# The samples' convolution, forget sums and value pages of a hybrid decoder step, moved to earlier places

## What is computed

```
mod = silu(c) @ w_mod + b_mod                      # six shift, scale and gate vectors
proj = modulate(rms(x)) @ w_in                     # columns: delta-rule heads, forgetting-attention heads
q,k,v = silu(causal_conv(proj[q,k,v], state_conv)) # 4 taps; samples: 3 older rows come from state_conv
o_gdn = gated_delta_chunked(l2norm(q), l2norm(k), v, g, beta, state_delta)
s = fq . fk / 8 + F_q - F_k ; F = cumsum(log forget)   # over all 2048 cached tokens and the new one
o_fox = softmax(s) @ v                             # samples: cached pages through page_table
x = x + g1 * ([o_gdn, o_fox] @ w_out)
x = x + g2 * peer(modulate(rms(x)))                # 8 heads x 16 experts per token, gathered rows of u and v
```

## Time and profile before

| | |
|---|---|
| median of three runs | 2023.49 us |
| the profiled execution's own time | 2020.36 us |
| its span, first to last instruction | 2017.2 us |
| TensorE busy, share of the span | 1651.2 us, 82% |
| VectorE busy | 1344.7 us, 67% |
| GpSimd busy | 816.4 us, 40% |
| ScalarE busy | 675.8 us, 34% |
| DMA | 722.49 MB, mean 358 GB/s |
| mean granted TensorE clock | 0.916 of full speed |

### The profile page before, as it was taken

How to read it: one execution, slowest core, us unless ns; L and a number is a source line. 1 busy time by engine, 2 the same in 40 slices (tenths; PEclk the granted TensorE clock), 3 DMA queues, 4 the chain that set the end, 5 groups by cost and what they waited for, 6 DMA issues and landing times.

```text
span 2017.2 us, 26386 instructions
## 1 busy us (share of the span) xinstructions
PE 1651.2 (82%) x8416; PEld 886.5 (44%) x8416; DVE 1344.7 (67%) x3103; ACT 675.8 (34%) x1971; POOL 816.4 (40%) x602
## 2 busy tenths in 40 slices
PE   6997989987968897776799787679978888887776
PEld 4444456654655553343355244335533443332233
DVE  4245767653468876666887666688768677775754
ACT  2111232121134452333445333344533333442332
POOL 0188664213014443343444234444434443444441
PEclk9998999987989997899899879889978999999999
DMA  7378657975679999999999999999999999999996
GB/s 309 111 261 286 223 172 242 320 240 189 204 304 418 420 417 423 422 421 421 406 391 406 423 413 422 421 401 402 392 415 405 422 421 419 420 422 421 420 408 276
DMA packets 130437, 722.49 MB, mean 358 GB/s; under 512 B 17288, under 2 KB 19017, under 8 KB 58357
## 3 DMA queue, kind: packets, MB, share of 16 engines
q0 software_dynamic: 75024, 545.82, 65.7%
q1 hardware_dynamic: 55277, 175.00, 24.1%
HBM read 711.77 MB, written 9.09 MB: 357 GB/s over the span
## 4 chain that ended last, share of the span: by engine, by line
PE 36%; DMA 31%; DVE 14%; issue 7%; SPq 5%; POOL 4%; ACT 3%; DVEq 0%; POOLq 0%; ACTq 0%
PE bank L493 35%; DMA R<-in_peer_uv,R 17%; DMA RING<-in_peer_uv,R 11%; DVE RING L2299 3%; SPq L2570 2%; SPq L2624 2%; DVE R L2299 2%; POOL MV L2486 1%; PE bank L500 1%; ACT R L1407 1%; DMA R<-in_x_prompt 1%; POOL R L2486 1%; POOL R L2556 1%; DMA RING<-samp_d 1%; ACT R L1417 1%
## 5 line engine op out<-in xcount | busy, mean ns | idle before, releaser
L2556 POOL DMA_INDIRECT RING<-in_peer_uv,R x390 | 442.2, 1134 | 663.5 <-PE bank L493 541.1
L493 PE MATMUL bank<-RING,R 128*64 128x512 f32 (+2 forms) x1560 | 516.7, 668 | 190.2 <-ACT R L1407 177.8
L2299 DVE SCALAR_TENSOR_TENSOR RING<-RING,MV 128x1024 f32<-128x1024 f32 x288 | 351.7, 1223 | 186.1 <-DMA RING<-in_peer_uv,R 167.0
L493 PE MATMUL bank<-R 128*128 128x128 f32 (+6 forms) x2184 | 404.5, 385 | 80.4 <-ACT R L1407 69.4
L493 PEld LDWEIGHTS bank<-R 128*128 128x128 f32 (+3 forms) x2184 | 261.2, 188 | 246.3 <-issue 236.5
L493 PEld LDWEIGHTS bank<-RING,R 128*64 128x64 f32 (+2 forms) x1560 | 159.0, 161 | 446.0 <-issue 433.8
L1417 ACT ACTIVATE R<-R 128x2 f32<-128x2 f32 x256 | 51.9, 203 | 705.5 <-DVE RING L2299 562.2
L2556 POOL DMA_INDIRECT R<-in_peer_uv,R x130 | 153.8, 1183 | 218.7 <-PE bank L493 200.9
L2299 DVE SCALAR_TENSOR_TENSOR RING<-RING,R 128x1024 f32<-128x1024 f32 x96 | 117.3, 1222 | 57.3 <-DMA RING<-in_peer_uv,R 49.7
L2299 DVE SCALAR_TENSOR_TENSOR R<-R,MV 128x1024 f32<-128x1024 f32 x96 | 117.5, 1224 | 55.2 <-DMA R<-in_peer_uv,R 49.2
L493 PE MATMUL bank<-HT,RING 128*128 128x512 f32 x320 | 140.7, 597 | 0.0
(11 more groups left out here) (340 smaller groups left out, 1888.7 us busy)
## 6 DMA issues: line engine op xcount, KB each, us to landing
R<-in_peer_wq SPq DMA_DIRECT2D x12, 2048.0 KB
RING<-in_w_mod SPq DMA_DIRECT2D x11, 2048.0 KB, 9.8
MV<-in_cache_k SPq DMA_DIRECT2D x88, 256.0 KB, 3.9
R<-in_cache_v SPq DMA_DIRECT2D x84, 256.0 KB, 3.6
R<-in_w_out SPq DMA_DIRECT2D x6, 2048.0 KB
MV<-in_cache_v SPq DMA_DIRECT2D x44, 256.0 KB, 3.8
R<-in_cache_k SPq DMA_DIRECT2D x40, 256.0 KB, 3.6
RING<-in_peer_uv,R POOLq DMA_INDIRECT x390
```

Of the source, the lines that this page charges most:

```text
L493: i = nc.tensor.matmul(out, lhsT, rhs, start=start, stop=stop, **k)
L2299: V.scalar_tensor_tensor(u, u, 1.0, H2HIGH if s_ % 2 and n < PAIRED * PH else H2[n // PH % 2], ALU.mult, ALU.mult, accum_out=DOT[:, n % 4, ...
L2556: nc.gpsimd.indirect_dma_start(UV[g % UN], None, a["peer_uv"][0], bass.IndirectOffsetOnAxis(ap=idx, axis=0)).then_inc(S(f"uv_in{g % UN}"), 16)
```

## The change

- **Samples' convolution.** It moves from GpSimd to VectorE, and from 8 rows of 512 columns to four blocks of 32 rows (8 used) of 128 columns. The weights and older rows are laid out so in two new inputs, zero in the unused rows, and loaded once, after the samples' rows of x. ScalarE copies the raw columns with one instruction (PSQ) for each of q, k, v. `sample_taps` (behind key group 4) multiplies and adds the older three rows, `sample_conv` (unit 1) adds the newest; silu comes at unit 2.
- **Forget sums.** TensorE's transposes and sums go before the fq projection and behind it; VectorE's parts stand behind key groups 0, 6, 7, 8, 9, 10 and 11.
- **New scores.** They are made behind key group 14; TensorE spreads them and the new log forgets with products by ones (`new_rows`), and VectorE copies them in convolution block 9. The trip through DRAM goes.
- **Softmax and values.** `sample_scores` comes at unit 0, `sample_probs` at 8, value group 0 at unit 10, up to group 15 at 25; groups 16 to 31 keep their places. SRULE_AT begins at 7 instead of 16.
- **SyncE.** Value groups 0 and 1 are loaded right behind the modulation biases; `sample_state_in` stands before `next_mod(5)`, ahead of the loop.
- **Tails.** TensorE's `tail_turns` and VectorE's `tails_out` stand ahead of the loop instead of in unit 0.

```diff
-SRULE_AT = (16, 19, 22, 25, 29)
+SRULE_AT = (7, 10, 13, 16, 20)
...
-        SCW = part(R2, 0, 2048, n=4, c=512)
-        SST = part(R2, 10760, 1536, n=3, c=512)
-        PSC = R2[:, 9224:9224 + CONV]
+        SCW = part(R2, 9216, 1536, j=TAPS, c=3 * P)
+        SST = part(R2, 10760, 1152, j=3, c=3 * P)
+        PSQ = part(R2, 8704, 384, n=3, c=P)
+        PSC = part(R2, 5696, 384, n=3, c=P)
...
-            return 18 + n if n < 16 else FOX_STEPS + (max(0, (n - 16) // 2 - 1) if LATE == 1 else (n - 16) * 7 * LATE // 16)
+            return 10 + n if n < 16 else FOX_STEPS + (max(0, (n - 16) // 2 - 1) if LATE == 1 else (n - 16) * 7 * LATE // 16)
...
+            forget_turns()
...
+                if name == "fq":
+                    forget_sums()
...
+            def new_rows():
+
+                pe.wait_ge(S("new_rows"), 2)
+                b = take_bank("new", "D")
+                mm(b[:, 0:64], ones[0:NB, :], NEW_LOGF.rearrange("p b h -> p (b h)"))
+                mm(b[0:1, 64:128], ones[0:NB, 0:1], NEW_SCORE.rearrange("p h b -> p (h b)"), sem=full("new"))
...
-            steps = {0: tail_turns, 1: forget_turns, 3: forget_sums, 10: sample_max_turn, 12: sample_max_spread, 16: sample_sums}
+            steps = {1: sample_max_turn, 3: sample_max_spread, 7: sample_sums}
...
+            tail_turns()
...
-                sample_rows((name, 4), g * 512, ACT.Copy)
-                act.sem_inc(S("sample_raw"), 1)
+                b = full_bank(act, (name, 4))
+                A(PSQ[:, g, :], b[:, 0:P], ACT.Copy).then_inc(S("sample_raw"), 1)
+                act.wait_ge(S("sample_raw"), g + 1)
+                act.sem_inc(free((name, 4)), 1)
...
-                if u == 12:
-
-                    act.wait_ge(S("sconv_done"), 3)
-                    A(PSC[0:NB, :], PSC[0:NB, :], ACT.Silu).then_inc(S("sconv_silu"), 1)
-                if u == 14:
+                if u == 2:
+                    act.wait_ge(S("sconv_done"), 1)
+                    A(PSC, PSC, ACT.Silu).then_inc(S("sconv_silu"), 1)
+                if u == 5:
...
+            def forget_pages(last, first):
+
+                for g in range(last, first - 1, -1):
+                    settle()
+                    step(V.tensor_tensor(TP[:, :, :, g], TP[:, :, :, g], TP[:, :, :, g + 1], ALU.add))
+
+            def forget_total():
+
+                settle()
+                step(V.tensor_tensor(flat(LP[:, :, :, 0:15]), flat(LP[:, :, :, 0:15]), flat(TP[:, :, :, 1:16]), ALU.add))
...
+            def sample_taps():
+
+                dve.wait_ge(S("sconv_in"), 32)
+                step(V.tensor_tensor(SST, SST, SCW[:, 0:3, :], ALU.mult))
+                for j in (1, 2):
+                    settle()
+                    step(V.tensor_tensor(SST[:, 0, :], SST[:, 0, :], SST[:, j, :], ALU.add))
+
+            def new_scores():
+
+                dve.wait_ge(S("sample_cols"), 12)
+                T8 = CACT[0:NB, 0, :]
+                step(V.tensor_tensor(T8, PS[0:NB, COL_FQ:COL_FQ + 512], PS[0:NB, COL_FK:COL_FK + 512], ALU.mult))
+                settle()
+                step(V.tensor_reduce(SN[0:NB, :], T8.rearrange("p (h d) -> p h d", h=8), AXX, ALU.add))
+                settle()
+                V.tensor_tensor(NEW_SCORE, SN[0:NB, :].rearrange("p (h o) -> p h o", o=1).to_broadcast([NB, 8, NB]),
+                                ident[0:NB, 0:NB].rearrange("p (o b) -> p o b", o=1).to_broadcast([NB, 8, NB]), ALU.mult).then_inc(S("new_rows"), 1)
+
+            among_keys = {0: forget_turned, 4: sample_taps, 6: forget_after, 7: lambda: forget_pages(14, 12), 8: lambda: forget_pages(11, 9),
+                          9: lambda: forget_pages(8, 5), 10: lambda: forget_pages(4, 0), 11: forget_total, 14: new_scores}
             for n in range(KEYS_BEFORE - 1):
                 key_group(n)
+                if n in among_keys:
+                    among_keys[n]()
             b = full_bank(dve, "gab")
             step(V.tensor_copy(GATE[:, 0:4, :], b[:, 0:4 * GATES_W].rearrange("p (t h) -> p t h", h=GATES_W)))
...
+            V.tensor_tensor(NEW_LOGF, ident[0:NB, 0:NB].rearrange("p (b o) -> p b o", o=1).to_broadcast([NB, NB, 8]),
+                            LOGF[0:NB, 4:5, :].to_broadcast([NB, NB, 8]), ALU.mult).then_inc(S("new_rows"), 1)
...
+                if cb == 9:
+                    b = full_bank(dve, "new")
+                    step(V.tensor_copy(LNB, b[:, 0:64]))
+                    dve.wait_ge(S("scores_cleared"), 1)
+                    V.tensor_copy(SC[0:1, :, :, 16], b[0:1, 64:128].rearrange("p (h b) -> p h b", h=8)).then_inc(free("new"), 1)
+                    job_read(dve, "new")
...
+            def sample_conv():
+
+                dve.wait_ge(S("sample_raw"), 3)
+                step(V.tensor_tensor(PSC, PSQ, SCW[:, 3, :].rearrange("p (n c) -> p n c", n=3), ALU.mult))
+                settle()
+                V.tensor_tensor(PSC, PSC, SST[:, 0, :].rearrange("p (n c) -> p n c", n=3), ALU.add).then_inc(S("sconv_done"), 1)
...
-            between = {0: tails_out, 1: forget_turned, 2: new_scores, 3: forget_after, 4: lambda: forget_pages(14, 12), 5: lambda: forget_pages(11, 9),
-                       6: lambda: forget_pages(8, 5), 7: lambda: forget_pages(4, 0), 8: forget_total, 9: sample_scores, 11: sample_max, 13: sample_shift, 15: sample_exp_sums, 17: sample_probs, 26: first_squares, 30: lambda: norm_sums(0), 32: srule_gate, 33: lambda: norm_scale(0)}
+            between = {0: sample_scores, 1: sample_conv, 2: sample_max, 3: write_decays, 4: sample_shift, 6: sample_exp_sums, 8: sample_probs,
+                       24: srule_gate, 26: first_squares, 30: lambda: norm_sums(0), 33: lambda: norm_scale(0)}
...
-            def sample_conv(g):
-
-                pool.wait_ge(S("sconv_in"), 32 * (g + 1))
-                pool.wait_ge(S("sample_raw"), g + 1)
-                step(T(SCONV(g), SRAW(g), SCW[0:NB, 3, :], ALU.mult))
-                for j in range(3):
-                    step(T(SST[0:NB, j, :], SST[0:NB, j, :], SCW[0:NB, j, :], ALU.mult))
-                    step(T(SCONV(g), SCONV(g), SST[0:NB, j, :], ALU.add))
-                pool.sem_inc(S("sconv_done"), 1)
...
+            load(SST, a["state_conv_rows"], "sconv_in")
+            load(SCW, a["conv_w_rows"], "sconv_in")
...
+            for n in range(2):
+                cache_group("cache_v", 32 + n, page_numbers(n))
+            store(o["conv_sample"][0, :, 0:2], a["state_conv"][0, :, 1:3], "samples_out")
             sp.wait_ge(S("sample_raw"), 3)
-            store(o["conv_sample"][0, :, 0:2], a["state_conv"][0, :, 1:3], "samples_out")
-            store(o["conv_sample"][0, :, 2], PS[0:NB, 0:CONV], "samples_out")
...
-            next_mod(4)
-            sp.wait_ge(S("new_score"), 1)
-            store(sgate_d[2], SN[0:NB, :], "samp_out")
-            for sem in ("samp_out", "samples_out"):
-                sp.wait_ge(S(sem), stored[sem])
-            load(LNB, o["logf_sample"][0, :, 0].rearrange("(o b) h -> o (b h)", o=1).to_broadcast([P, 64]), "new_in")
...
+            next_mod(4)
+            sp.wait_ge(S("tail_out"), 3)
+            store(o["conv_prompt"][0, 0], TAILO[0:3, :], "samples_out")
+            sample_state_in()
+            next_mod(5)
+            next_mod(6)
...
-                if z == 12:
-                    sample_state_in()
-                if z == 30:
+                if z == 22:
                     sp.wait_ge(S("srule"), 4)
                     store(o["delta_sample"][0].rearrange("b h k v -> (b h) (k v)"), SS0[0:64].rearrange("p k v -> p (k v)"), "srule_stored")
-                if z == 32:
+                if z == 26:
```

More of the change, by code:

```diff
@@ L286, in hybrid_decoder_step @@
         LNB = RQ64[:, 0:64]
+        NEW_LOGF = part(small, 896, 64, b=NB, h=8)[0:NB]
+        NEW_SCORE = part(small, 960, 64, h=8, b=NB)[0:NB]
         M64 = RQ64[:, 64:128]
@@ L589, in _, with forget_turns, forget_sums @@
             last_job.append(newest[0])
+            def forget_turns():
+                pe.wait_ge(S("logf_pages"), 16)
+                for half in range(2):
+                    b = take_bank(("lp", half), "D")
+                    for m in range(4):
+                        h = half * 4 + m
+                        tr(b[:, m * P:(m + 1) * P], LG.rearrange("p (n h) -> p h n", h=HEADS)[:, h, :], full(("lp", half)) if m == 3 else None)
+            def forget_sums():
+                job_read(pe, ("lp", 0))
+                job_read(pe, ("lp", 1))
+                for half in range(2):
+                    rhs = SLOT2[:, 2112 + half * 512:2112 + half * 512 + 512]
+                    b = take_bank(("lsum", half), "D")
+                    mm(b[:, :], lower[:, :], rhs, sem=full(("lsum", half)))
+                    b = take_bank(("ltot", half), "D")
+                    mm(b[:, :], ones[:, :], rhs, sem=full(("ltot", half)))
+            forget_turns()
             for name in ("fq", "fk"):
@@ L656, in tail_turns @@
```

(44 more changed lines are left out.)

64 lines of the change are left out of this document (8 added, 56 removed).

## The result

The changed kernel takes 2032.7 us (median of 20 runs, 2023.8 to 2041.5), the kernel before 2024.0 (20 runs, 2017.7 to 2033.2). The ratio is 1.0041, with a 95% interval of 1.0025 to 1.0057: slower by 8 to 9 us, 0.4%. The profiled execution took 2030.8 us, its span 2028.9 against 2017.2.

A forecast was written before the change was run, and what follows sets the result against it. Key products and reduces bind until 190.9 us, later the values' pages; front delays reach the end. 2020.4 + 17.6 + 0 - 7.5 = 2030.5, called 2032 as median; range 2008 to 2044, the forecast's own 2025 to 2039, chance 0.42.

The forecast's parts named there:

- Place 1: Key groups up to reduce 17: VectorE's 21 added two-SBUF-input instructions wait for running GpSimd products; costs 17.6 us, +-5.
- Bound and path: Whole span: key products and reduces bind until 190.9 us; what the front of 600 us gains or loses moves the end equally.
- Copies out of PSUM and reduces show no such length: VectorE beside GpSimd products: these are not stretched, unlike tensor_tensor sums with both inputs in SBUF (4.54 us).
- those behind 10 meet products 11, 12 and 13: Page sums behind key group 10 wait for three products; reduce 11 ends near 181, product 14 starts 16.6 us late, about 187.
- TensorE's 16.9 us instead of 20 or more: At the gates: a sign of the forecast being right was TensorE waiting 20 us or longer for L1631's copy.
- the sums behind 8 and 9: Page sums behind key groups 8 and 9 run in GpSimd's wait for pages before product 11, at 0.3 us each.
- Rival A: Key groups: VectorE's work fits between the products, sums 0.27 us each; 2013, about 2014.5 as a median; chance 0.18.
- rival B: Key groups: waits exist but GpSimd's idle time for pages hides most, leaving some 7 us; 2020 to 2022; chance 0.2.
- Conv stage at zero: Between gates and attention loop: fewer ScalarE copies and tail turns moved ahead count zero at the loop's start (-1 to +2).
- Place 2: Attention loop, values from unit 10: turns 6.5 us earlier, plus -1 in the levels; -7.5 us in all, bounds 0 and -16.
- rival C: Key groups cost as forecast, but the values' move gives nothing, as SyncE holds unit 10 up; 2038 to 2040; chance 0.2.
- Levels: Gated-delta levels after the turns: one value turn and one head mask fewer, -1 us.

The follow-up runs named there:

- the single-input kernel: Against the changed kernel, the 21 VectorE instructions among the key groups read one SBUF input only (adding constant 0), results not the kernel's: 2036.2 us, one execution.
- the PSUM kernel: Against the changed kernel, the second input of the 21 VectorE instructions among the key groups comes from a PSUM bank, results not the kernel's: 2016.4 us, one execution.

## Why the prediction was right

The time was forecast at 2032 and came at 2032.7, and the mechanism of Place 1 is shown. The terms were off by up to 7 us, and their errors cancelled; that the total fits so closely is luck.

- **Bound and path.** Right: a later reduce 17 moves the gates' copy, the loop and the end by about as much.
- **Place 1, the mechanism.** Right, from both sides: moving the 21 instructions out of the products' way gives back 10.7 of the 10.9 us between first product and reduce 17, and taking only one operand out of SBUF gives 8.1. "Copies out of PSUM and reduces show no such length" held in all traces. That it was said of pairs of SBUF inputs alone was too narrow: the single-input kernel is held as well, 9.9 us against 10.9.
- **Place 1, the size: mis-sized.** 17.6 forecast, 10.7 measured (13.1 at the gates less the 2.4 of the start). With the start added, the steps came out so: reduce 5 ends at 138.0 forecast, 137.6 measured; product 8 at 143.8, 143.59 measured; product 11 at 166.3, 165.14 measured. The step that failed is "those behind 10 meet products 11, 12 and 13". The five sums took 5.38 us: one of them waited for product 11, then GpSimd itself waited 1.96 us for pages (171.61), and the other four ran in that gap. Product 14 came at 183.25 instead of 189.4, and the rest of the chain kept that difference. The wait of 1.71 us there, shorter than before the change, and TensorE's 16.9 us instead of 20 or more are the signs of it. I had charged a product per instruction there, though I had used such a gap for the sums behind 8 and 9.
- **Rival A** (all fits in the gaps) and **rival B** (some 7 us at most) fell: 2013 and 2020 to 2022 are outside the interval, and A's sums of 0.27 us were seen only where GpSimd waited. But B's price for Place 1, some 7 us, was nearer to the 10.7 than the forecast's 17.6: most of the waiting was hidden, as for the rows behind group 4, which lie in GpSimd's wait before product 8 and cost 2.6. B's time was missed because the start, the tails and Place 2 came out dearer than B had them from the forecast.
- **The start.** Not in the forecast: the first product is 2.4 us later after, and 1.6 to 3.3 later in the twelve traces that have the new loads. 2.2 of the 2.4 stand in TensorE's first stage before 54 us, ahead of the change's first instruction. Its 32 modulation products, before and after:

```profile
31.16 4.19 PE L493 MATMUL bank<-R,ident 128*128 128x128 f32 x32 [1.85 <-DVE R L1573]
```

```profile
31.20 5.79 PE L490 MATMUL bank<-R,ident 128*128 128x128 f32 x32 [1.85 <-DVE R L1584]
```

The mean granted clock from 31 to 38 us was 0.76 instead of 1.00, so part of them ran at the lower of the two levels. SyncE issues the first of the new loads only at 57.13, so they can't have caused this. From 38 to 54 us the mean clock was 0.89 in the trace of the kernel before and 0.71 to 0.79 in the twelve others, so the one trace of before may just have been a good one. In the PSUM kernel only 0.8 stand before 54 us, and 1.1 more come later, where SyncE issues the third key group (3.23 us instead of 1.89). With one trace of the kernel before, the start is not settled.
- **Conv stage at zero.** 4.0 measured. The tails moved ahead of the loop wait 3.63 us for a bank that VectorE frees. With the tails in unit 0 the 4 us are gone there, but the loop is longer by as much.
- **Place 2, mis-sized.** -6.5 to the turns forecast. From gates to turns it is 251.7 before and 252.3 after, so nothing is gained: the loop is 3.3 us shorter (145.2 to 141.9), and the 4.0 of the tails take that back. In the loop, value group 2 goes out 36.3 us after the first row maximum (38.4 forecast: right), the sixteenth is read 82.2 later (79: SyncE's pace is 5.6 us per group), and the turns follow 23.4 later (21: the 8 bare units, those without values, took 2.4 each instead of 2.2, from 435.1 to 454.4, and TensorE waits 2.12 us for VectorE's norm at the end). The move by itself is worth some 3 us, as the kernel with it undone shows, halfway between the forecast and rival C's "nothing". For the whole stretch from gates to turns C was nearer, but for another reason than its own: the tails, and not SyncE. Its time, 2038 to 2040, was not met, since Place 1 was smaller than in it.
- **Levels.** -1 forecast, 2.5 measured from the turns to the first dot (157.6 to 155.2); kernels with the same code there show 152.6 to 160.8, so this is not resolved.

The trace's terms: 2.4 + 10.7 + 0.7 - 2.5 = 11.3 at the first dot. The medians differ by 8.7; one execution of each kernel can't say more.

## What to carry to other kernels

Idle time of VectorE beside a GpSimd elementwise loop is not free room. In the key stage of these traces each VectorE sum, copy or scalar operation from SBUF to SBUF that met a running GpSimd product lasted until the product's end, down to a copy of 8x8; reduces and instructions with an operand in PSUM did not. Not all of that is lost: the 21 instructions were 34.7 us longer (43.5 against 8.8 with an operand in PSUM), and 8.1 of it showed at reduce 17; the rest fell into VectorE's idle time and GpSimd's waits for pages. It counts where VectorE frees the buffers that those pages wait for and GpSimd has no such wait left. Put such work where GpSimd waits or has not begun, and count the work's own length too: begun 1.6 us before the first product, 15 sums were worse than where they had stood, and begun 7.4 us before, they were free. Where it can't be moved, an operand in PSUM lets it through.

## What was not expected of the hardware

- An 8x8 copy from SBUF to SBUF took 4.47 us beside a product (after, at 205.15), and a 128x64 add of a constant three times 11.25 us. Reduces of 128x2048 from SBUF took 2.29 us beside products throughout, a reduce of 8x512 0.67.
- A two-input instruction with one operand in PSUM and its output in SBUF is not held: 128x64 sums of 0.29 us each.
- The Trainium skill (SBUF — State Buffer, "Who interferes with whom") says that a VectorE instruction with two SBUF inputs contends with a GpSimd one that reads SBUF, that copies, casts and tensor_scalar can enter modes that use both ports and then contend as well, and that a reduce never does on this chip. The trace agrees for the sums (12.60 us for three), the 8x8 copy (4.47), the scalar adds (11.25 for three) and the reduces (2.29 each). The prediction had drawn on the first of these alone.
